# Two halves of the tokens in turn around three layer norms of a decoder trunk, and buffers of its own for the last dense step

## The reference, cut to what matters

```
for l in range(2):
    mod = silu(c) @ w_mod[l] + b_mod[l]
    sh1, sc1, g1, sh2, sc2, g2 = split(mod, 6)
    h = x * (1 + sc1) + sh1
    y = hybrid_mixer(h, w_in[l], w_a2[l], b_a[l], gla_norm_g[l], w_out[l])
    x = layer_norm(ALPHA * x + (1 + g1) * y, ln_g[l, 0], ln_b[l, 0])
    h = x * (1 + sc2) + sh2
    y = swiglu(h, ...) if l == 0 else moe_swiglu(h, ...)
    x = layer_norm(ALPHA * x + (1 + g2) * y, ln_g[l, 1], ln_b[l, 1])
```

## Time and profile before

| | us |
|---|---|
| median of three runs | 1322.58 (1322.08 to 1323.61) |
| the profiled execution, own time | 1323.89 |
| its span | 1322.2 |
| TensorE's mean granted clock | 0.975 of full speed |

### The profile page before, as it was taken

How to read it: one execution, slowest core, us unless ns; L and a number is a source line. 1 busy time by engine, 2 the same in 40 slices (tenths; PEclk the granted TensorE clock), 3 DMA queues, 4 the chain that set the end, 5 groups by cost and what they waited for, 6 DMA issues and landing times.

```text
span 1322.2 us, 26435 instructions
## 1 busy us (share of the span) xinstructions
PE 1212.8 (92%) x11284; PEld 657.5 (50%) x11284; DVE 552.1 (42%) x841; ACT 312.4 (24%) x545; POOL 43.5 (3%) x84
## 2 busy tenths in 40 slices
PE   2988979999979887699999999999999999999996
PEld 1878867778858877423333333334333333333332
DVE  6898877777658997520021020020110210200224
ACT  0556133443236560220020020011110201200200
POOL 3100010000010000100000000000000000000001
PEclk9999979999989999799999999999999999999998
DMA  9954767899617549588999989989989989989850
GB/s 341 314 193 160 256 227 287 314 358 322 231 50 219 183 153 379 217 318 351 411 334 406 364 305 415 413 324 404 375 306 411 402 335 383 390 351 411 339 224 32
DMA packets 149083, 403.60 MB, mean 305 GB/s; under 512 B 19964, under 2 KB 71328, under 8 KB 137696
## 3 DMA queue, kind: packets, MB, share of 16 engines
q1 hardware_dynamic: 146720, 395.16, 79.9%
q0 software_dynamic: 2240, 6.68, 1.4%
HBM read 400.75 MB, written 1.05 MB: 304 GB/s over the span
## 4 chain that ended last, share of the span: by engine, by line
PE 67%; DVE 9%; issue 2%; DMA 1%; ACT 1%; POOL 0%; DVEq 0%; SPq 0%; ACTq 0%
PE bank L1284 34%; PE bank L1308 17%; PE bank L329 3%; PE bank L331 3%; PE bank L330 3%; PE bank L1318 2%; PE bank L1264 1%; DVE u_low L1508 1%; PE bank L1289 1%; DVE mod_acc L1497 1%; PE bank L1272 1%; DMA raw_u<-in_ffn_w_up_dram 1%; PE bank L1273 1%; PE bank L984 1%; DVE score L1567 1%
## 5 line engine op out<-in xcount | busy, mean ns | idle before, releaser
L1284 PE MATMUL bank<-raw_w,xg 128*32 128x512 f32 x4096 | 457.8, 593 | 1.1 <-issue 1.1
L1284 PEld LDWEIGHTS bank<-raw_w,xg 128*32 128x32 f32 x4096 | 126.7, 109 | 260.4 <-issue 258.2
L1308 PE MATMUL bank<-raw_w,heT 128*32 128x512 f32 x2112 | 232.9, 593 | 0.0
L1859 DVE TENSOR_TENSOR he<-he,bank 128x256 f32<-128x256 f32 x64 | 23.3, 417 | 384.5 <-ACT he L843 384.5
L1308 PEld LDWEIGHTS bank<-raw_w,heT 128*32 128x32 f32 x2112 | 66.9, 110 | 148.8 <-issue 147.6
L843 ACT ACTIVATE he<-bank 128x256 f32<-128x256 f32 (+1 forms) x72 | 21.4, 370 | 413.1 <-PE bank L1284 282.2
L1886 DVE SCALAR_TENSOR_TENSOR ycat<-bank,gate_tab,ycat 128x512 f32<-128x512 f32 x36 | 25.4, 747 | 184.7 <-PE bank L1273 182.8
L1497 DVE SCALAR_TENSOR_TENSOR mod_acc<-mod_row,c_act,mod_acc 128x1024 f32<-128x1024 f32 x70 | 89.9, 1284 | 9.6 <-DMA mod_row<-in_w_mod_dram 3.9
L329 PE MATMUL bank<-u_high,hT_H 128*128 128x256 f32 x256 | 75.1, 293 | 4.6 <-DVE u_low L1508 4.6
L331 PE MATMUL bank<-u_high,hT_L 128*128 128x256 f32 x256 | 72.8, 284 | 0.0
L330 PE MATMUL bank<-u_low,hT_H 128*128 128x256 f32 x256 | 72.7, 284 | 0.0
(11 more groups left out here) (292 smaller groups left out, 1497.8 us busy)
## 6 DMA issues: line engine op xcount, KB each, us to landing
raw_w<-in_moe_w_down_dram SPq DMA_DIRECT2D x88, 1024.0 KB, 8.3
raw_w<-in_moe_w_gate_dram SPq DMA_DIRECT2D x128, 512.0 KB, 7.3
raw_w<-in_moe_w_up_dram SPq DMA_DIRECT2D x128, 512.0 KB, 8.6
mod_row<-in_w_mod_dram SPq DMA_DIRECT2D x80, 512.0 KB, 6.6
raw_w<-in_moe_w_gate_dram SPq DMA_DIRECT2D x64, 384.0 KB, 3.8
raw_w<-in_moe_w_up_dram SPq DMA_DIRECT2D x64, 384.0 KB, 5.0
...
```

What stands on the lines that cost most here:

```text
L1284: last = mm(bank[m // 4][32 * q:32 * q + 32, :].rearrange("s (m f) -> s m f", m=2), xg[:, i, k, 32 * g:32 * g + 32], W[:, :, a * 256:(a + ...
L1308: last = mm(bank[3 + g][32 * q:32 * q + 32, :], heT[:, i, at:at + 32], W[:, b, h * 512:(h + 1) * 512], start=(c == 0 and a == 0), stop=(c ...
L1859: last = V.tensor_tensor(he[:, b, :], he[:, b, :], bank[b][:, 256:512], ALU.mult)
```

## The change

For ph = 0, 1, 2 each half of the tokens is transposed on its own (`transposed_tile`, 8 transposes, feature tiles 4 to 7 first, into banks of `TOKEN_BANK`) as soon as it is normalised. ACT modulates tiles 4 to 7 of a half (in `normalise`, 128x128 each), DVE tiles 0 to 3 (`modulate(ph, t)`), DVE after the statistics of both halves. The consumers (`gate_up_plain`, the first unit of mixer 1, the router) work half by half and take tiles 4 to 7 first, with half 1's transposes in the midst of half 0's work. The last two output units of a mixer are made for half 0, then for half 1, and the terms of half 0 wait for a semaphore of their own (`wo`). The last `down` step gets its own buffers (`d10_H`, `d10_L`, `hidT10_H`, `hidT10_L`), is split up earlier, and PE finishes half 0 of steps 9 and 10 before half 1. At ph = 0 the conditioning sum and ln_mod are made between the halves. At ph = 2 gate3's apply follows the statistics, `norm_out(2)` moves as a whole behind `gate_tab`, and `xH1`, `xL0` get places that `norm_out` does not read, so ACT's wait for it goes.

The core of the diff:

```diff
+TOKEN_BANK = {1: ((1, 2), (4, 5)), 2: ((0, 1), (2, 3)), 3: ((1, 2), (0, 3))}
+KT_ORDER = (4, 5, 6, 7, 0, 1, 2, 3)
...
+        d10_H = place("d10_H", [P, 2, D], F32R, at=over - 24 * 1024)
+        d10_L = place("d10_L", [P, 2, D], F32R, at=over - 16 * 1024)
+        hidT10_H = place("hidT10_H", [P, 2, 2, P], F32R, at=over + 24 * 1024)
+        hidT10_L = place("hidT10_L", [P, 2, 2, P], F32R, at=over + 26 * 1024)
...
-        xH1 = place("xH1", [P, D], F32R, at=rows_at + 4096)
-        xL0 = place("xL0", [P, D], F32R, at=rows_at + 8192)
+        xH1 = place("xH1", [P, D], F32R, at=over + 32 * 1024)
+        xL0 = place("xL0", [P, D], F32R, at=over + 36 * 1024)
...
+                    act.wait_ge(s["lnm"], ph + 1)
+                    act.wait_ge(s["xT_ps"], 4 * (ph + 1) + 2 * t + 1)
+                    b = bank[TOKEN_BANK[ph + 1][t][1]]
+                    for kt in range(4, KT):
+                        A(hfull[:, kt, t * P:(t + 1) * P], b[:, (kt - 4) * P:(kt - 3) * P], ACT.Identity,
+                          scale=ln_mod[:, ph, 0, kt:kt + 1], bias=ln_mod[:, ph, 1, kt:kt + 1]).then_inc(s["hfull_a"], 1)
...
+                if q == STEPS - 1:
+                    dense_conv_d(q, d10_H)
...
                 act.wait_ge(s["xb_ps"], i + 1)
-                if t:
-                    act.wait_ge(s["x_ln"], 6)
...
+            def transposed_tile(ph, t):
+
+                pe.wait_ge(s["x_n"], 2 * ph + t - 1)
+                for b in (1, 0):
+                    for i in range(4):
+                        kt = 4 * b + i
+                        last = nc.tensor.transpose(bank[TOKEN_BANK[ph][t][b]][:, i * P:(i + 1) * P],
+                                                   ycat[:, t, kt * P:(kt + 1) * P], ident[:])
+                    last.then_inc(s["xT_ps"], 1)
...
+                    if l and u == U_BQ:
+                        for t in range(TT):
+                            tok = slice(t * P, (t + 1) * P)
+                            for ct in range(2):
+                                for kt in KT_ORDER:
+                                    if ct == 0:
+                                        token_tile(2 * l, t, kt)
+                                    last = mm(b[:, ct * T + t * P:ct * T + (t + 1) * P], u_raw[u % 4][:, kt, ct * P:(ct + 1) * P],
+                                              hfull[:, kt, tok], start=(kt == KT_ORDER[0]), stop=(kt == KT_ORDER[-1]))
+                                if t == 0 and ct == 0:
+                                    transposed_tile(2 * l, 1)
...
-                for i in (2, 3):
-                    project_out(l, i, range(4, 8))
-                    project_out(l, i, range(0, 4))
-                    if l == 0:
-                        m = i + 1
-                        pe.wait_ge(s["row_rd"], (m - 1) * KT)
-                        sum_chunk(mod_acc[m % 2], bank[3 * (i - 2)][:, 0:KT]).then_inc(s["mod_ps"], 1)
-                    elif i == 2:
-                        pe.wait_ge(s["row_rd"], len(MOD_ROWS))
-                        gate_sum(11, (0, 3))
+                for t in range(TT):
+                    for i in (2, 3):
+                        project_out(l, i, range(4, 8), (t,))
+                        project_out(l, i, range(0, 4), (t,))
+                        if l == 0 and i == 2 + t:
+                            m = i + 1
+                            pe.wait_ge(s["row_rd"], (m - 1) * KT)
+                            sum_chunk(mod_acc[m % 2], bank[3 * t][:, 0:KT]).then_inc(s["mod_ps"], 1)
+                        elif l and t and i == 2:
+                            pe.wait_ge(s["row_rd"], len(MOD_ROWS))
+                            gate_sum(11, (0, 3))
...
+                        if t == 0 and i == 0 and kt == KT_ORDER[3]:
+                            transposed_tile(1, 1)
...
+            q, p = STEPS - 1, STEPS - 2
+            pe.wait_ge(s["f_hid"], 2 * q + 1)
+            pe.wait_ge(s["f_tL"], 2 * p + 1)
+            hidden_transposes(0, bank[4]).then_inc(s["f_t"], 1)
+            for t in range(2):
+                pe.wait_ge(s["f_tL"], 2 * p + 1 + t)
+                for j in range(2):
+                    pe.wait_ge(s["f_dL"], 2 * p + j + 1)
+                    down(t, j, ybank[t], False, None).then_inc(s["f_d"], 1)
+                if t == 0:
+                    pe.wait_ge(s["f_hid"], 2 * q + 2)
+                    pe.wait_ge(s["f_tL"], 2 * p + 2)
+                    hidden_transposes(1, bank[7]).then_inc(s["f_t"], 1)
+                    pe.wait_ge(s["row_rd"], ROWS_MIX1)
+                    gate_sum(9, (0, 1))
+                pe.wait_ge(s["f_tL"], 2 * q + 1 + t)
+                for j in range(2):
+                    pe.wait_ge(s["f_dL"], 2 * q + j + 1)
+                    down(t, j, ybank[t], False, j == 1).then_inc(s["f_d"], 1)
...
+            pe.wait_ge(s["small_ld"], 32)
+            for t in range(TT):
+                for kt in KT_ORDER:
+                    token_tile(3, t, kt)
+                    last = mm4(bank[(7, 5)[t]][:, 0:NE], hfull[:, kt, t * P:(t + 1) * P], wr[:, kt, :],
+                               start=(kt == KT_ORDER[0]), stop=(kt == KT_ORDER[-1]))
+                if t == 0:
+                    tokens_back(0)
+            last.then_inc(s["rt_ps"], 1)
...
+            def modulate(ph, t):
+
+                dve.wait_ge(s["xT_ps"], 4 * ph + 2 * t + 2)
+                b = bank[TOKEN_BANK[ph][t][0]]
+                for kt in range(4):
+                    V.tensor_scalar(hfull[:, kt, t * P:(t + 1) * P], b[:, kt * P:(kt + 1) * P], ln_mod[:, ph - 1, 0, kt:kt + 1],
+                                    ln_mod[:, ph - 1, 1, kt:kt + 1], ALU.mult, ALU.add).then_inc(s["hfull"], 1)
...
                     V.bn_aggr(mv[:, t, :], stats[:, t]).then_inc(s["mv"], 1)
-                if ph < 3:
-                    if ph == 0:
+                    if ph == 0 and t == 0:
                         dve.wait_ge(s["mod_ps"], 4)
                         conditioning(0, 4, bank[3][:, 0:KT]).then_inc(s["modT"], 1)
                         dve.wait_ge(s["modT"], 4)
                         norm_and_modulation(0)
-                    if ph == 2:
-                        norm_out(2, (0,))
-                    modulate(ph + 1)
-                    if ph < 2:
-                        low_of_tokens(ph + 1)
-
-            def norm_out(ph, ts=range(TT)):
-
-                for t in ts:
+                if ph == 2:
+                    gate_apply(11, (0, 3), gate3_row)
+                for t in range(TT):
+                    modulate(ph + 1, t)
+                if ph < 2:
+                    low_of_tokens(ph + 1)
+
...
-                        dve.wait_ge(s["proj"], l * NU + NIN + 3 + h)
+                        dve.wait_ge(s["proj" if t else "wo"], l * NU + NIN + 3 + h if t else 2 * l + 1 + h)
...
+                    dense_low_d(p, d_L, d_H)
+                    dve.wait_ge(s["f_tH"], 2 * p + 2)
+                    hidden_low(1, 7, hidT_L, hidT_H)
+                if q == STEPS - 1:
+                    dense_low_d(q, d10_L, d10_H)
+                dve.wait_ge(s["f_silu"], 2 * q + 2)
...
+            dve.wait_ge(s["f_tH"], 2 * STEPS)
+            hidden_low(1, 7, hidT10_L, hidT10_H)
+            gate_apply(9, (0, 1), g_row)
...
-                dve.wait_ge(s["f_d"], 4 * STEPS - (2 if t == 0 else 0))
+                dve.wait_ge(s["f_d"], 4 * STEPS - (4 if t == 0 else 0))
...
-            norm_out(2, (1,))
...
                 last = V.tensor_tensor(gate_tab[:, :, 1 + p * NE:1 + (p + 1) * NE], gate[:], tmp[:], ALU.add)
+            norm_out(2)
```

203 lines of the change are left out of this document (101 added, 102 removed).

## The result

The changed kernel takes **1303.97 us** (median of 4, 1301.91 to 1308.08) against 1322.33 for the kernel before on the same chips: a ratio of 0.9865, 95% interval 0.9837 to 0.9893. That is faster by 1.1 to 1.6%. The forecast was 1303.2. The profiled execution took 1303.0 (span 1301.3); before it was 1323.9 (span 1322.2).

What follows compares the result with a forecast made beforehand. PE is busy 92% of the span, so time can only come from its idle stretches, led by waits at three layer norms. Gains 3.7 + 5.9 + 9.8 = 19.4 us give 1303.2 us as a median, range 1298 to 1310.

Steps and rivals of the forecast that it cites:

- A: Layer norm between mixer 0 and dense layer: working the token halves in turn gains 3.7 us, lower end 0.4.
- The conditioning: In A, the small conditioning work moved between the halves delays half 1's normalise by 0.7 us.
- B: Layer norm between dense layer and mixer 1: halves in turn gain 5.9 us, lower end 1.2, upper end 7.1.
- the unit load behind the rows: In B, the unit load queued on SP behind modulation rows 64 and 65 goes out 5.9 us earlier, setting the gain.
- what follows shifts as a block: Assumption under the sum: the three places' gains add up as long as later work shifts as a block.
- C: Layer norm between mixer 1 and router: halves in turn and norm_out(2) moved start the gather 9.8 us earlier; ends 8, 11.5.
- rival 3: Half-split does less in C: terms(1) and POOL as slow as before, C gains 8.0, total 1305.0 us; chance 0.10.
- Rival 1: PE stays at the low clock where now busy in short pieces: gain 14.3, total 1308.3 us; chance 0.15.
- Rival 2: Row loads behind norm_out lead in dense layer and mixer 1: gain 14.3, total 1308.3 us; chance 0.10.
- Rival 4: Slower: PE's low clock is held past the three places, total 1331 us; chance 0.02.
- The rule against this: Transposes not counting as PE-busy would keep PE's clock low longer with the split; judged less likely from the rows.

Runs made afterwards that it cites:

- the fifth run: Changed kernel with SyncE issuing modulation rows 64 and 65 behind the load of unit 6 instead of ahead of it: 1304.9 us.
- the repetition: The changed kernel timed and profiled once more without any edit: 1306.9 us, ratio to the kernel before 0.9843-0.9885.
- the second experiment: Changed kernel with B put back: steps 9 and 10 each do both halves in turn, both halves normalised before the first transpose: 1311.0 us.
- the third experiment: Changed kernel with C's halves put back: mixer 1's projection unit by unit, both halves normalised before the first transpose, norm_out(2) still moved: 1308.0 us.

## Why the prediction was right, point by point

**A, 3.7: measured 3.64.** The conditioning cost 0.65 (0.7), the passes end 25.51 behind terms(0) (25.4), and undoing A alone gives 29.8. Two errors hide in the size: DVE's 128x128 step took 0.34 (I took 0.30), ScalarE's 0.38 (0.33). The sum of the record does not quite close either: its own steps end the passes at 190.5 with the second transposes at the full clock (gain 4.0) and at 191.4 with them at the low one (3.1), and 3.7 lies between. So the exact value is luck, and more so as where the clock rises differs from one execution to the next: 24.4 in three profiles with the changed A and no constants in it, 25.3 to 25.6 in five. (With the constants it is 24.4 each time.)

**B, 5.9: measured 6.04 at K.** Every step is in the rows: terms(0) 3.9 earlier (3.7), the projection's end 6.9 (7.1), the unit load behind the rows 5.9 (5.9; the earlier trace rows 411.97, now 400.09, each against `hid`). That this load leads and not DVE was shown by the fifth run. The step that failed is the one under the sum, that what follows shifts as a block: mixer 1 took 0.7 more from K to F. In the first profile that is one wait of DVE for a modulation row, which the kernel before does not have:

```profile
471.93 1.29 DVE L1578 SCALAR_TENSOR_TENSOR mod_acc<-mod_row,c_act,mod_acc 128x1024 f32<-128x1024 f32 x1 [0.81 <-DMA mod_row<-in_w_mod_dram]
```

In the repetition it is 2.4 more, 1.7 of it by the clock over the gate's sum. The forecast had no term for either.

**C, 9.8: measured 9.26.** Half 1 normalised 7.34 earlier (7.4). From its normalise to the gather 13.88 instead of 15.80: 1.9 where I had 2.5. The low clock is not the miss, for the sum had it in. From that normalise to the router's last record it took 6.3 where the sum had 5.95, and from the routing's first step to the gather 7.5 where before it took 7.3 (528.98 less 521.49; 549.52 less 542.18). POOL's L579 was 0.24 and 0.22 and ScalarE followed in 1.28: rival 3 is out.

**The sum** of 19.4 stands against 18.9 in the three places. The forecast's own time for the profiled execution, 1304.5, came out 1303.0, since the start was 1.8 and the experts 1.1 quicker, neither of them in a place of the change; by all nine executions the median is 1304.9, so the forecast of 1303.2 was 1.7 low. Undoing everything gives back 18.5.

**The rivals.** Rival 1, PE at the low clock where it works in short pieces, came true in C (0.50 from 516 to 524, and the gather) and in A, as I had it in their prices, and not in B, where I had placed it: in the first profile the clock never fell there. In the second experiment, with the halves together, it fell again (eight transposes in 1.97); and in two profiles with the changed B it fell as well, once at a cost of 1.6 us and once at none (last section). Rival 2: the rows' loads led in B, as forecast, and for 0.8 us at one place behind K. Rival 4: nothing of the kind was seen; the experts took 1.1 us less than before, not more.

**The rule against this.** The Trainium skill (TensorE: Matmul & The Clock Gate, Part 4: PE-mode transpose) says that transposes do not count as PE-busy for the clock as matmuls do. Here two profiles speak against it. PE's timeline of the third experiment:

```profile
522.55 3.68 PE L982 MATMUL bank<-ident,ycat 128*128 128x128 f32 x16 [7.33 <-ACT ycat L700]
526.16 0.77 PE L963 MATMUL bank<-wr,hfull 128*32 128x8 f32 x64
```

Sixteen transposes at the low clock, 0.23 each, after 7.3 us idle, and the next 64 router records take 0.77 where they take 1.04 at the low clock and 0.72 at the full one. The clock was back at once, after transposes alone. In the changed kernel 8 transposes, 64 router records, 4 transposes and 64 records took from 516.49 to 521.4 at the low clock all the way. So more matmuls did not raise it sooner; which stretch is low was not to be read from the kind of the instruction.
